# Two transformer stacks on one core: other start addresses, modulo 512 bytes, for the weights and activations that TensorE reads

## The reference

```python
def first_block(...):
    for i in range(2):
        hl, hc = _modulate(x, ml[0], ml[1]), _modulate(xc, mc[0], mc[1])
        if i == 0:
            yl, yc = _mlstm_mixer(hl, hc, True, m_w_up, m_conv_w, m_conv_b, m_w_qk, m_w_v, ..., m_w_og, m_norm_g, m_w_out)
        else:
            yl, yc = _mla_mixer(hl, hc, False, ang, a_w_dq, a_q_norm, a_w_uq, a_w_dkv, a_kv_norm, a_w_ukv, a_w_out)
        x = _layer_norm(ALPHA * x + ml[2] * yl, ln_g[i, 0], ln_b[i, 0])
        x = _layer_norm(ALPHA * x + ml[5] * _conv_ffn(_modulate(x, ml[3], ml[4]), ...), ln_g[i, 1], ln_b[i, 1])
        # the same two lines for xc in layer 0
    return x

def _conv_ffn(h, w_in, conv_w, conv_b, w_out):
    gate, up = jnp.split(h @ w_in, 2, axis=-1)            # 1024 -> 2 x 2816
    return (jax.nn.silu(_dwconv(gate, conv_w, conv_b)) * up) @ w_out

def second_block(x, ...):
    for l in range(2):
        zc = jnp.split(modulate(rms_norm(h_ctx, norm1_g[l]), ...) @ w_in[l], 10, axis=-1)
        zx = jnp.split(modulate(rms_norm(x, norm1_g[l]), ...) @ w_in[l], 10, axis=-1)
        x = x + mod_x[2] * token_mixers(zx, k1, k2, v, *mix_args)          # ends in @ w_out[l]
        x = x + mod_x[5] * channel_mixer(modulate(rms_norm(x, norm2_g[l]), ...), mlp_w1[l], mlp_w2[l])
        # l == 0: the same for h_ctx
    return rms_norm(x, final_g)
```

## Time and profile before

| | before |
|---|---|
| median of 3 runs | 2488.53 us (2488.27 to 2494.13) |
| profiled execution, its own time | 2484.04 us |
| its span | 2482.3 us |
| TensorE busy | 2379.6 us, 96% of the span |
| VectorE busy | 1652.8 us, 67% |
| ScalarE busy | 987.2 us, 40% |
| TensorE matmuls | 12204 |
| mean granted TensorE clock | 0.982 |

### The profile page before, as it was taken

How to read it: one execution, slowest core, us unless ns; L and a number is a source line. 1 busy time by engine, 2 the same in 40 slices (tenths; PEclk the granted TensorE clock), 3 DMA queues, 4 the chain that set the end, 5 groups by cost and what they waited for, 6 DMA issues and landing times.

```text
span 2482.3 us, 30985 instructions
## 1 busy us (share of the span) xinstructions
PE 2379.6 (96%) x12204; PEld 1937.1 (78%) x12204; DVE 1652.8 (67%) x2686; ACT 987.2 (40%) x1534; POOL 30.7 (1%) x64
## 2 busy tenths in 40 slices
PE   7999999999999999999998998999999999988997
PEld 3878877866677888887758997766788888767997
DVE  6776567345368886778558778487666565677664
ACT  2422232236443321223554444465432232456543
POOL 0000000010000000000000000000000000000000
PEclk9999999999999999999999999999999999999999
DMA  8355534452153445343404553211245345323553
GB/s 320 110 189 203 187 136 159 180 215 91 68 191 116 144 155 192 131 157 104 149 20 139 190 183 128 68 51 51 93 154 211 136 164 191 100 74 113 180 188 126
DMA packets 95803, 357.16 MB, mean 144 GB/s; under 512 B 10969, under 2 KB 11353, under 8 KB 93353
## 3 DMA queue, kind: packets, MB, share of 16 engines
q1 hardware_dynamic: 93082, 339.37, 39.0%
q0 software_dynamic: 2576, 15.82, 1.8%
HBM read 349.90 MB, written 5.24 MB: 143 GB/s over the span
## 4 chain that ended last, share of the span: by engine, by line
PE 72%; issue 16%; DVE 8%; ACT 3%; DMA 1%; POOL 0%; SPq 0%; POOLq 0%; DVEq 0%; ACTq 0%
PE PS L545 57%; PE PS L573 3%; PE PS L707 3%; PE PS L902 2%; DVE w_lo L1633 1%; PE PS L1065 1%; ACT w_hi L1090 1%; PE PS L825 1%; PE PS L843 1%; PE PS L818 1%; DVE conv L2281 1%; DMA ada_ring<-in_ada 1%; DVE ada_ring L1649 0%; PE PS L660 0%; ACT wgt L1221 0%
## 5 line engine op out<-in xcount | busy, mean ns | idle before, releaser
L1633 DVE TENSOR_TENSOR w_lo<-raw,w_hi 128x1024 fp32r<-128x1024 f32 (+1 forms) x456 | 543.3, 1209 | 341.1 <-ACT w_hi L1090 339.7
L1090 ACT ACTIVATE w_hi<-raw 128x1024 fp32r<-128x1024 f32 (+1 forms) x456 | 461.1, 1041 | 475.9 <-PE PS L545 466.4
L545 PE MATMUL PS<-h_hi,w_hi 128*128 128x512 f32 (+1 forms) x1432 | 485.5, 339 | 17.4 <-DVE h_lo L1742 9.0
L545 PE MATMUL PS<-h_lo,w_hi 128*128 128x512 f32 (+1 forms) x1432 | 484.1, 338 | 0.0
L545 PE MATMUL PS<-h_hi,w_lo 128*128 128x512 f32 (+1 forms) x1432 | 483.7, 338 | 0.0
L545 PEld LDWEIGHTS PS<-h_hi,w_hi 128*128 128x128 f32 x1432 | 270.6, 189 | 50.8 <-issue 12.8
L545 PEld LDWEIGHTS PS<-h_lo,w_hi 128*128 128x128 f32 x1432 | 270.5, 189 | 30.5 <-issue 0.2
L545 PEld LDWEIGHTS PS<-h_hi,w_lo 128*128 128x128 f32 x1432 | 270.7, 189 | 29.9
L545 PE MATMUL PS<-hid_hi,w_hi 128*128 128x512 f32 (+1 forms) x864 | 290.1, 336 | 2.8 <-DVE w_lo L1633 2.8
L545 PE MATMUL PS<-hid_lo,w_hi 128*128 128x512 f32 (+1 forms) x864 | 290.1, 336 | 0.0
L545 PE MATMUL PS<-hid_hi,w_lo 128*128 128x512 f32 (+1 forms) x864 | 289.1, 335 | 0.0
(11 more groups left out here) (366 smaller groups left out, 3608.2 us busy)
## 6 DMA issues: line engine op xcount, KB each, us to landing
raw<-in_weights SPq DMA_DIRECT2D x434, 512.0 KB, 4.5
ada_ring<-in_ada SPq DMA_DIRECT2D x176, 512.0 KB, 3.7
raw<-in_weights SPq DMA_DIRECT2D x22, 384.0 KB, 4.0
qk<-in_ada SPq DMA_DIRECT2D x4, 1024.0 KB, 10.7
xv<-in_ada SPq DMA_DIRECT2D x4, 1024.0 KB, 12.8
m_hi<-h_spill POOLq DMA_DIRECT2D x4, 1024.0 KB, 7.8
wgt<-in_x SPq DMA_DIRECT2D x2, 1024.0 KB, 22.4
h_spill<-h_hi POOLq DMA_DIRECT2D x1, 2048.0 KB, 8.9
```

What stands on the lines that cost most here:

```text
L545: mm = pe.matmul(out, a, b, start=(k == 0 and i == 0), stop=(k == ph.k_tiles - 1 and i == 2))
L1090: act.activation(w_hi[:, s, 0:w], raw[:, s, 0:w], ACT.Copy).then_inc(sem("w_hi"), 1)
L1633: dve.tensor_tensor(w_lo[:, s, 0:w], raw[:, s, 0:w], w_hi[:, s, 0:w].bitcast(F32), ALU.subtract)\
```

## The change

The 32-byte allocation and the spacer helper give way to an allocation with a chosen alignment (`line`), and tiles are put elsewhere modulo 512:

- The small tiles (`mod_dot` to `eps`) are allocated first, and `raw` behind them with alignment 512. `raw`, `w_hi`, `w_lo`, `ada_ring`, `ada_junk` and `crow` come to 0 (128 before).
- `xv`, `h0_hi`, `h0_lo`, `m_hi`, `m_lo`, `hs`, `qk`, `wgt` and `og` come to 0 (192 before).
- `gap_h` is 480 bytes behind a line of 512: `h_hi`, `h_lo`, and behind them `ckv`, `cq`, `z` and the other small products come to 480 (192 before).
- `gap_hid` is 32 bytes behind a line: `hid_hi`, `hid_lo` come to 32 (192 before).
- Where only latents are computed, the operand is packed: `packed(tensor, i)` takes the tile as one flat row and puts slice i at column 16 + 256 i, so the slices lie one behind the other, 1024 bytes each, and 64 bytes behind the tile's start. For `h` that is 32 modulo 512, for `hid` 96. It holds for `aout`, f1, `wo1` and g1, in the producers (ScalarE, VectorE) and the consumer. The latent slices of an `h` that was made for 512 columns or is read beside such a product (`dq`, `zg1`, `z1`) stay in place, at 480.

No instruction, wait, queue or size is added, removed or moved on any engine; only addresses differ. The diff, cut:

```diff
+OFF_LINE = 16
-        def sb(name, shape, dt=F32, stack=ctx):
-            return stack.enter_context(nc.sbuf_tensor(name, shape, dt))
-        def behind_line(name, gap, stack):
-            stack.enter_context(nc.sbuf_tensor(name, [P, gap // 4], F32, align_bytes=LINE))
+        def sb(name, shape, dt=F32, stack=ctx, line=32):
+            return stack.enter_context(nc.sbuf_tensor(name, shape, dt, align_bytes=line))
...
-        raw = sb("raw", [P, RING, UNIT])
-        w_hi = sb("w_hi", [P, RING, UNIT], F32R)
...
         eps = sb("eps", [P, 1])
+        raw = sb("raw", [P, RING, UNIT], line=LINE)
+        w_hi = sb("w_hi", [P, RING, UNIT], F32R)
+        w_lo = sb("w_lo", [P, RING, UNIT], F32R)
...
-            m_hi = sb("m_hi", [P, 16, T], F32R, st)
+            m_hi = sb("m_hi", [P, 16, T], F32R, st, LINE)
...
-                m_lo = sb("m_lo", [P, 16, T], F32R, inner)
+                m_lo = sb("m_lo", [P, 16, T], F32R, inner, LINE)
...
-            behind_line("gap_h", 192, st)
+            sb("gap_h", [P, 120], F32, st, LINE)
             h_hi = sb("h_hi", [P, 8, T], F32R, st)
             h_lo = sb("h_lo", [P, 8, T], F32R, st)
             with ExitStack() as inner:
+                sb("gap_hid", [P, 8], F32, inner, LINE)
                 hid_hi = sb("hid_hi", [P, 16, T], F32R, inner)
...
+        def packed(tensor, i):
+            flat = tensor[:].rearrange("p t n -> p (t n)")
+            return flat[:, OFF_LINE + i * CTX:OFF_LINE + (i + 1) * CTX]
+
+        def columns_at(tensor, i, full, cols=slice(0, T)):
+            return tensor[:, i, cols] if full else packed(tensor, i)
...
-            hx = lambda full: (lambda k: h_hi[:, k, rng(full)], lambda k: h_lo[:, k, rng(full)])
-            hid = lambda full: (lambda k: hid_hi[:, k, rng(full)], lambda k: hid_lo[:, k, rng(full)])
+            hx = lambda full: (lambda k: columns_at(h_hi, k, full), lambda k: columns_at(h_lo, k, full))
+            hl = (lambda k: h_hi[:, k, LAT], lambda k: h_lo[:, k, LAT])
+            hid = lambda full: (lambda k: columns_at(hid_hi, k, full), lambda k: columns_at(hid_lo, k, full))
...
-            residual_product("aout", *hl, False, True, ready=[("att_e", 16), ("o_lo", 7)], each=("o_lo", 0))
+            residual_product("aout", *hx(False), False, True, ready=[("att_e", 16), ("o_lo", 7)], each=("o_lo", 0))
...
-                    linear("zg1", *hx(False))
+                    linear("zg1", *hl)
...
-                y_hi, y_lo = (lambda p: z_hi(Y_ORDER[p])), (lambda p: z_lo(Y_ORDER[p]))
+                y_hi, y_lo = (lambda p: y_part[0](Y_ORDER[p])), (lambda p: y_part[1](Y_ORDER[p]))
...
-                        act.activation(hid_hi[:, f, r], TMP[:, 4 + f % 2, r], ACT.Copy).then_inc(sem("hid_hi"), 1)
+                        act.activation(columns_at(hid_hi, f, full), TMP[:, 4 + f % 2, r], ACT.Copy).then_inc(sem("hid_hi"), 1)
...
-                        dve.tensor_tensor(hid_lo[:, f, r], TMP[:, 4 + f % 2, r], hid_hi[:, f, r].bitcast(F32), ALU.subtract)\
+                        dve.tensor_tensor(columns_at(hid_lo, f, full), TMP[:, 4 + f % 2, r], columns_at(hid_hi, f, full).bitcast(F32), ALU.subtract)\
```

More of the change, by code:

```diff
@@ L298, in two_stacks @@
         eps = sb("eps", [P, 1])
+        raw = sb("raw", [P, RING, UNIT], line=LINE)
+        w_hi = sb("w_hi", [P, RING, UNIT], F32R)
+        w_lo = sb("w_lo", [P, RING, UNIT], F32R)
+        ada_ring = sb("ada_ring", [P, ADA_RING, D])
+        ada_junk = sb("ada_junk", [P, D])
+        crow = sb("crow", [P, 2, D])
         with ExitStack() as st:
@@ L876, in _ @@
                 if l:
-                    front(("zg1",), *hx(False), ("h_lo", 8 * 6))
-                    linear("zg1", *hx(False))
+                    front(("zg1",), *hl, ("h_lo", 8 * 6))
+                    linear("zg1", *hl)
                     linear("kv1", *hx(True))
@@ L887, in _ @@
                 per_head = len(slots) // 4
-                z_hi, z_lo = hx(full)
+                z_hi, z_lo = hx(True) if full else hl
+                y_part = hx(full)
                 def z_tile(step):
@@ L1305, in h_tiles @@
                     for i, (c, v) in enumerate(halves(full)):
-                        ins = act.activation(h_hi[:, t, c], TMP[:, t % 4, c], ACT.Identity,
+                        ins = act.activation(columns_at(h_hi, t, full, c), TMP[:, t % 4, c], ACT.Identity,
                                              bias=mod[:, par, 8 * chunk + t, v:v + 1])
@@ L1349, in hi @@
                         act.wait_ge(sem("prod"), base - 44 + i + 1)
-                        act.activation(hid_hi[:, i, r], TMP[:, 4 + i % 2, r], ACT.Copy).then_inc(sem("hid_hi"), 1)
+                        act.activation(columns_at(hid_hi, i, full), TMP[:, 4 + i % 2, r], ACT.Copy).then_inc(sem("hid_hi"), 1)
                     def relu(i, t):
@@ L1415, in o_hi @@
                 act.wait_ge(sem("att_o"), h + 1)
-                act.activation(h_hi[:, h, LAT], PS[:, out_bank(h), 0:CTX], ACT.Copy).then_inc(sem("o_hi"), 1)
+                act.activation(columns_at(h_hi, h, False), PS[:, out_bank(h), 0:CTX], ACT.Copy).then_inc(sem("o_hi"), 1)
             only_split("uqr")
@@ L1527, in y_hi @@
                         act.wait_ge(sem("y_made"), 6 * l + min(p, 5) + 1)
-                    act.activation(h_hi[:, Y_ORDER[p], r], TMP[:, p % 4, r], ACT.Copy).then_inc(sem("y_hi"), 1)
+                    act.activation(columns_at(h_hi, Y_ORDER[p], full), TMP[:, p % 4, r], ACT.Copy).then_inc(sem("y_hi"), 1)
                 for at, i in enumerate(Z_STEPS[l]):
@@ L2015, in lo @@
                     for c, v in halves(full):
-                        ins = dve.scalar_tensor_tensor(out=h_lo[:, t, c], in0=TMP[:, t % 4, c], scalar=scalar(par, chunk, t, v),
-                                                       in1=h_hi[:, t, c].bitcast(F32), op0=ALU.add, op1=ALU.subtract)
+                        ins = dve.scalar_tensor_tensor(out=columns_at(h_lo, t, full, c), in0=TMP[:, t % 4, c], scalar=scalar(par, chunk, t, v),
+                                                       in1=columns_at(h_hi, t, full, c).bitcast(F32), op0=ALU.add, op1=ALU.subtract)
                     ins.then_inc(sem("h_lo"), 1)
@@ L2169, in o_lo @@
                 dve.wait_ge(sem("o_hi"), h + 1)
-                dve.tensor_tensor(h_lo[:, h, LAT], PS[:, out_bank(h), 0:CTX], h_hi[:, h, LAT].bitcast(F32), ALU.subtract)\
+                dve.tensor_tensor(columns_at(h_lo, h, False), PS[:, out_bank(h), 0:CTX], columns_at(h_hi, h, False).bitcast(F32), ALU.subtract)\
                     .then_inc(sem("o_lo"), 1)
@@ L2350, in y_lo @@
                     j = Y_ORDER[p]
-                    dve.tensor_tensor(h_lo[:, j, r], TMP[:, p % 4, r], h_hi[:, j, r].bitcast(F32), ALU.subtract)\
+                    dve.tensor_tensor(columns_at(h_lo, j, full), TMP[:, p % 4, r], columns_at(h_hi, j, full).bitcast(F32), ALU.subtract)\
                         .then_inc(sem("y_lo"), 1)
```

3 lines of the change are left out of this document (1 added, 2 removed).

## The result

The change did next to nothing, and what it did was to cost a little. The kernel after takes 2495.76 us (median of 17 runs, 2491.68 to 2499.67); 17 runs of the kernel before, taken beside them, have a median of 2490.99 (2484.27 to 2498.50). The ratio is 1.002, with a 95% interval of 1.0012 to 1.0028. The profiled execution took 2493.65 us with a span of 2491.9, against 2484.04 and 2482.3 before. The forecast was 2461.5 us, 27 us under the 2488.5 shown of before. The time lies inside the stated range of 2427 to 2504 us, but that range held both signs; the forecast was a gain, and a small loss came.

What follows compares the result with a forecast made beforehand. TensorE's matmul stream was taken as the bound; -11.8 - 8.7 - 7.8 = -28.3 us, about 95% reaching the end, gave -27 us from 2488.5, so 2461.5 us. Range 2427 to 2504 us.

Steps and rivals of the forecast that it cites:

- What bounds the kernel: In most stages, some 1600 us of the span, TensorE sets the time and nothing else is near its limit.
- The step that failed: Float32r matmuls: pitch grows in steps of 4.4 ns, one per 512-byte line the moving slice crosses, one sometimes covered.
- The third support: Product z, first mixer in block two: 233.3 ns, one 4.4 ns step over f0 at the same values modulo 512.
- Term 1: First mixer at 0, 2688 matmuls: one step of 4.4 ns less, -11.8 us; bounds -23.7 to +11.8.
- Term 2: `h` and `hid` with 512 columns at 480 and 32, 3960 matmuls: half a step less, -8.7 us; bounds -17.4 to +17.4.
- Term 3: Packed 256 columns: f1 and `aout` one step faster, -7.8 us, g1 stays; bounds -21.2 to +6.8.
- Slower: Rival: a crossing 8 columns from an edge of `h` and `hid` costs a step, g1 slows; 2500 to 2511 us, chance 0.24.
- A: The forecast's theory for float32r matmuls: the 512-byte lines that the moving slice crosses set the pitch.
- The change does nothing: Rival: steps come from the moving data's rate and weight-load rhythm, not slice starts; 2488 us, chance 0.20.
- Deeper: Rival: one more crossing covered in all forms, some 42 us at the end; 2446 us, or 2435; chance 0.18.
- What would show it: Pitch by stage: 224.5 ns in `up`, 229 in `v`; `v` at 233 and `up` at 229 clears lines, f0 at 233 means edge costs.

Runs made afterwards that it cites:

- sweep1: Computation replaced by chains of 48 float32r matmuls on TensorE alone over a grid of both start addresses; 226.7 to 234.2 ns with 512 columns, 113.3 to 120.0 with 256.
- first_part: Kernel before with only the weights and the first mixer moved to 0, `h` and `hid` left at 192 and unpacked; 2485.24 us, ratio 0.998.
- all_shifted_128: packed_at_192 with every operand, weights too, 128 bytes further, all distances the same; 2464.66 us, ratio 0.9887.
- wide_at_zero: Kernel after with `h` and `hid` of 512 columns at 0, packed slices left at 32 and 96; 2472.23 us, ratio 0.9916.
- packed_at_192: all_at_zero with the packed 256-column slices started at 192; 2458.84 us, ratio 0.9872.
- second_part: Kernel before with only the later operands moved (`h` at 480, 32 packed; `hid` at 32, 96 packed), weights and first mixer unmoved; 2508.04 us, ratio 1.007.
- all_at_zero: Kernel after with `h`, `hid` and the packed slices at 0 too; 2478.99 us, ratio 0.9951.
- sweep2: Chains as in sweep1, with other entries, fewer stationary or moving columns, or bf16; bf16 216.0 ns with 512 columns, float32r at 256 columns 117.8 or 113.3 at equal addresses.

## Why the prediction was wrong, point by point

**What bounds the kernel: right.** TensorE's stream set the time in the same stages, and nothing became late beside it: VectorE went from 67 to 66% and ScalarE stayed at 40%. One row was passed over: PEld, the weight loads, is at 184.03 of 185 us in f1. Its records overlap, so that is no rate, but "nothing else is near its limit" left out the very operand that the reading missed. And the 16 records of the earlier trace rows are eight matmuls in two passes (the trace has 96 records for the 48 matmuls of L747), so 429 ns is one pass; the 2.6 ns are per pass, and nothing else hangs on it.

**The step that failed** is the sentence "My reading is that the steps belong to 512-byte lines of the moving operand". It was a ladder of four values (1 to 4 times 4.4 ns) read as a count of lines. The differences were real; what they counted wasn't. Two of the four rungs (f1 and g1) were one distance in two paces; the other two, 229.0 and 233.3, were two distances, 64 in f0 and g0 and 192 in `v`, for which sweep1 has 228.9 and 233.3. The operand that the reading left out, the stationary one, moved in the same change from 128 to 0. One comparison in the trace of before pointed there: f0 moves a slice at 192 over weights at 128 and takes 229.0, `v` moves weights at 128 over `m` at 192 and takes 233.3. Same two addresses, roles exchanged; I took it for a rhythm. The third support, product z one step over f0, was one chain out of a mixture, see below. What the runs show in place of the lines is the distance between the two operands: in first_part the weights alone move under f0, and its pitch goes from 229.0 to 233.2; in all_shifted_128 no operand is on a line, and 226.7 stays.

**Term 1, the first mixer (-11.8 us).** 1536 matmuls of `up`, `qk`, `mout` went from 228.9 to 226.7 and 1152 of `v` and `og` from 233.3 to 226.7: 1536 x 2.2 + 1152 x 6.6 = 11.0 us less. The size is luck: the step of 4.4 lies halfway between two others, 2.2 and 6.6.

**Term 2, `h` and `hid` with 512 columns (-8.7, bounds -17.4 to +17.4).** f0 and g0 went to 233.3: 3960 x 4.4 = +17.4 us, just the far bound. Here the whole forecast turned. Of two ends that "nothing in the trace tells" apart I took a value for what seemed likelier; distances of 224 and 32 are among the worst, and a gain was to be had only at 0.

**Term 3, 256 columns (-7.8, bounds -21.2 to +6.8).** f1 and `aout`: 720 matmuls on `h` at 116.6 gain 1.2 ns each, the other 528 on `h` stay at 117.8, and 528 on `hid` lose 2.3, about 0 in all. g1: 768 x 4.4 + 768 x 6.6 = +8.4 us. This lies over the upper bound, which knew of no pace above 117.8. wide_at_zero shows the same packed slices without term 2: it is 13.4 us over packed_at_192.

**The sum.** -11.0 + 17.4 + 8.4 = +14.8 us; measured +4.8 between the medians and +9.6 between the profiled executions. Part of the rest may be the clock. The granted clock of each run has a mean of 0.981 in the 33 runs of the kernel before that stand beside the experiments and of 0.984 in the 17 of the kernel after (0.9812 and 0.9836). Between its levels of 1.2 and 2.4 GHz that is 2 x 0.0188 x 2491 = 94 us at the lower one before and 2 x 0.0164 x 2496 = 82 us after. If TensorE has work all that time, half of the 12 us is saved, 6 us. The runs themselves say less: a line through the 33 runs has 1.2 us for 0.001 of clock, and this estimate 2.5. So the column is an upper estimate. All variants have it:

| kernel | by pitches, us | by clock, us | sum | measured |
|---|---|---|---|---|
| after | +14.8 | -6.0 | +9 | +4.8 |
| first_part | +6.4 | -5.7 | +1 | -5.5 |
| second_part | +27 | -5.0 | +22 | +17.3 |
| all_at_zero | -5.9 | -8.5 | -14 | -11.8 |
| wide_at_zero | -12 | -8.0 | -20 | -19.2 |
| all_shifted_128 | -17 | -7.0 | -24 | -26.8 |
| packed_at_192 | -28 | -10.7 | -39 | -32.4 |

(The pitches are those of the stretches times the counts of the prediction; the clock is each kernel's mean over its runs against 0.9812.) Pitch and clock together come to within 7 us each time, or within some 9 with half the clock. The order of the variants is that which was measured, but the pitches alone give it too; they are 4 to 12 us too long in all seven, and whether the clock is all of that no run shows. Why the clock is granted a little more of the time, in slower and in faster variants alike, no run tells.

**The rivals.** "Slower" had its consequence right: f0 at 233 ns, g1 slower, the first mixer's gain beside it, 2500 us. That is 4 us over the 2495.8 measured. Its mechanism, a line 8 columns from an edge, fell with A: first_part has f0 at 233.2 with no such edge. Its figure on g1 was short by what distance 96 costs, and it knew nothing of the clock. "The change does nothing" comes nearest in the change itself (0 against +4.8, where "slower" had +12.4) and is wrong in every large stage; in time "slower" is nearer, as the base is 2.5 us higher beside this measurement. "Deeper" is ruled out for this change; its gain of 42 to 53 us was reached by no variant, though packed_at_192 takes 32 us off by addresses alone.

**What would show it.** The list did its work. It said that f0 at 233 means the edge costs, and that `v` staying at 233 and `up` at 229 would clear the lines. Both went to 226.7, and A was false all the same: no entry asked for a move of the weights under resting `h`, the one test that separates the two operands.

**What stays open.** Product z in block two is at distance 64, where sweep1 and sweep2 have 228.9 with 512 columns after every entry. Of its 16 chains before, three ran at 233.3 (that of the earlier trace rows is one) and the others at 228.7 to 230.2, so 512 columns too have two paces there, which the sweeps never met. In the kernel after, at distance 224, all are near 233. And which of its two paces a 256-column stage takes can't be told beforehand: f1 of first_part has distance 192 and 117.8 ns, f1 of packed_at_192 the same distance and 113.2. How the two operands' addresses come to act on each other inside the chip is open too.

## What to carry to other kernels

When a TensorE-bound stage of float32r matmuls has a pitch over its columns, write down both start addresses of each pair, modulo 256, and not only that of the operand you mean to move; an edit that moves the weights changes every product in the kernel. A ladder of equal steps in a trace is a pattern, not a cause: 96 chains of 48 matmuls over a grid of both addresses took 0.86 ms of chip time and would have named 0 for 512 columns and 192 for 256 (113.3 or 117.8 there) at once. And where the two ends of a term's bounds differ in sign and no row decides, the forecast hangs on that term, however well the others are worked out.

## What the runs showed of the hardware

- Float32r matmuls of 512 columns and 128 stationary columns have a pitch of 226.7 to 234.2 ns, by the distance of the two start addresses modulo 256, on a grid of 32 bytes (sweep1); 256 columns 113.3 to 120.0 ns. The best distance of the one (0) is a bad one of the other (120.0).
- Starts off the 32-byte grid of the kernel go on in the same way in sweep2: with 512 columns 234.7 ns at distance 4, 233.3 at 8, 231.7 at 16; with 256 columns 123.3, 119.3 and 116.7.
- With bf16 the pitch is 216 and 109 ns, for 512 and 256 columns, at distances 0, 32, 64 and 192. With float32r the distance matters at 128 and at 64 stationary columns, a little at 32 (256 columns: 117.8 ns at distance 0, 113.3 at 64 and 192; 512 columns 231.7 at all three) and hardly at 16. The records of the weight loads go the same way: 188 ns for 128 columns of float32r, 134 for 64, 108 for 32, 94 for 16, and 98 for 128 of bf16. So the runs do not part the size of an element from the length of a load. That the reads of the next weights and of the moving slice get in each other's way fits all of it, but was not tried by itself: 16 columns are not faster than 128 at distance 0, so it isn't simply the bytes read.
- From 512 to 384 to 256 moving columns the pitch falls by 53 ns each time (226.7, 173.3, 120.0 at distance 0), and from 256 to 128 only to 111.7. So 113.3 ns for 256 columns seems to be near a floor that the moving columns don't set. Whether the load of the 128 stationary columns does, no chain tried.
- With 256 columns, distances 64 and 192 have two paces 4.5 ns apart. What ran ahead of a chain can decide between them (four transposes or two, at the same addresses), but no rule for it came out: at 192 two transposes gave both. In the sweeps the choice holds for the chain's 48 matmuls; f1 of all_shifted_128 changed from 113.2 to 118 ns on its way.
